# The delta rule's outputs kept token by token instead of feature by feature

## What is computed

```python
def step(s, xs):                      # one chunk of 64 tokens, per head, per direction
    qd, kd, u_c, w_c, qk_c, al = xs   # qd = q * exp(cumsum(log decay))
    v_new = u_c - w_c @ s
    o = qd @ s + qk_c @ v_new
    s = s * al + kd.T @ v_new
    return s, o

def finish(o_pair, gate):             # the two directions' outputs, latent tokens only
    o = rms_norm(o_pair[0] + o_pair[1], norm_g)     # over the 128 features of a head
    return (o * silu(gate)) @ w_out
```

## Time and profile before

| | |
|---|---|
| runs shown | 3884.72, 3899.01, 3894.75 us; median 3894.75 us |
| profiled execution | span 3889.4 us from the first to the last instruction; no separate time is given for it |
| TensorE busy | 3713.0 us, 95% |
| VectorE, ScalarE, GpSimd busy | 50%, 39%, 22% |
| mean granted TensorE clock | 0.980 |
| first scan, second chunk stage, second scan | about 255 to 461, 461 to 595, 595 to 804 us |
| gate, output projection | about 804 to 871, 871 to 919 us |

### The profile page before, as it was taken

One profiled execution on the slowest core, in us unless ns is written; L12 is line 12 of the kernel. 1 busy time (PEld: TensorE's weight loads), 2 busy tenths in 40 slices (PEclk: granted clock), 3 DMA queues, 4 the chain that ended last, 5 costly groups with the idle time before them and its releaser, 6 DMA issues.

```text
span 3889.4 us, 60956 instructions
## 1 busy us (share of the span) xinstructions
PE 3713.0 (95%) x25674; PEld 3011.8 (77%) x25674; DVE 1933.2 (50%) x2996; ACT 1516.2 (39%) x2548; POOL 845.8 (22%) x842
## 2 busy tenths in 40 slices
PE   6999899999999999998999999999999899999999
PEld 4678787987888757786888788876778688878887
DVE  6656555535444565745243543447565533454343
ACT  5533233323323356735233432235575522343222
POOL 1222122121111133442110120203344321002120
PEclk8999999989999999999999999999999999999999
DMA  6310030012222202111224122221111122222222
GB/s 240 121 43 3 19 70 3 3 64 105 97 96 96 71 28 76 61 60 49 94 96 137 63 93 98 98 82 39 66 60 60 35 96 98 103 92 98 95 96 91
DMA packets 81543, 300.88 MB, mean 77 GB/s; under 512 B 8824, under 2 KB 9976, under 8 KB 80504
## 3 DMA queue, kind: packets, MB, share of 16 engines
q1 hardware_dynamic: 80240, 294.90, 21.8%
q10 hardware_dynamic: 1032, 2.10, 0.5%
HBM read 292.76 MB, written 4.19 MB: 76 GB/s over the span
## 4 chain that ended last, share of the span: by engine, by line
PE 74%; DVE 11%; ACT 6%; issue 5%; POOL 3%; DMA 1%; SPq 0%; DVEq 0%; POOLq 0%; ACTq 0%
PE ps L208 73%; DVE wlo L239 1%; DVE he L247 1%; ACT whi L227 1%; DVE ac L247 1%; PE ps L213 1%; ACT ha L227 1%; POOL p L243 1%; DVE hc L2476 1%; ACT L227 1%; ACT wp L228 1%; DVE ss L247 1%; DVE ws L247 1%; DVE ha L239 1%; DVE sml L1944 0%
## 5 line engine op out<-in xcount | busy, mean ns | idle before, releaser
L239 DVE TENSOR_TENSOR wlo<-wraw,whi 128x1024 fp32r<-128x1024 f32 x537 | 689.8, 1289 | 777.4 <-ACT whi L227 776.7
L208 PE MATMUL ps<-hh,whi 128*128 128x512 f32 x1840 | 732.0, 398 | 6.5 <-ACT hh L227 2.1
L208 PE MATMUL ps<-hl,whi 128*128 128x512 f32 x1840 | 722.6, 393 | 0.0
L208 PE MATMUL ps<-hh,wlo 128*128 128x512 f32 x1840 | 722.0, 392 | 0.0
L227 ACT ACTIVATE whi<-wraw 128x1024 fp32r<-128x1024 f32 x537 | 559.6, 1049 | 207.7 <-PE ps L208 171.8
L208 PEld LDWEIGHTS ps<-hh,whi 128*128 128x128 f32 x1840 | 348.9, 190 | 90.9 <-ACT hh L227 7.7
L208 PEld LDWEIGHTS ps<-hh,wlo 128*128 128x128 f32 x1840 | 349.1, 190 | 74.2
L208 PEld LDWEIGHTS ps<-hl,whi 128*128 128x128 f32 x1840 | 349.5, 190 | 70.2
L208 PE MATMUL ps<-u,u 64*64 64x64 f32 (+2 forms) x6016 | 223.7, 226 | 25.5 <-DVE u L239 15.4
L208 PEld LDWEIGHTS ps<-u,u 64*64 64x64 f32 (+1 forms) x6016 | 204.7, 137 | 41.6 <-DVE u L239 19.4
L239 POOL TENSOR_TENSOR sml<-sml,con 128x4 f32<-128x4 f32 (+3 forms) x36 | 66.4, 1847 | 640.3 <-DVE sml L244 579.1
(11 more groups left out here) (402 smaller groups left out, 7062.6 us busy)
## 6 DMA issues: line engine op xcount, KB each, us to landing
wraw<-weights SPq DMA_DIRECT2D x537, 512.0 KB, 3.2
x<-xT SPq DMA_DIRECT2D x2, 2048.0 KB, 9.5
bias_lines<-ln ACTq DMA_DIRECT2D x1, 2048.0 KB
xmf<-memT SPq DMA_DIRECT2D x2, 1024.0 KB, 4.7
out<-x SPq DMA_DIRECT2D x4, 512.0 KB, 2.6
bias<-bias_lines SPq DMA_DIRECT2D x1, 1536.0 KB, 8.3
con<-consts SPq DMA_DIRECT2D x1, 1379.0 KB, 16.5
ctxt<-ctxT SPq DMA_DIRECT2D x1, 1024.0 KB, 18.4
```

The lines of the kernel that those rows point to most:

```text
L208: self.last, self.open = self.e.matmul(out, lhsT, rhs, start=start, stop=stop, skip_group_check=skip), True
L239: return self.e.tensor_tensor(out, a, b, op)
```

## The change

Outputs are now made with tokens on the partitions. The q product uses q itself as the weights and the state as the moving operand, into the rows of its chunk; the decay is applied afterwards, as a scale per partition on ScalarE while it leaves PSUM (into `EQ`), and GpSimd adds it to `OT`. The score product goes to a PSUM bank of its own, one for both directions. `OT` is laid out by unit pair (`place`), with 128 tokens by 512 features. The squares of head group 0 are made in the q steps of the second chunk stage, on ScalarE, and summed in the free dimension on VectorE; GpSimd takes the root and normalizes. Those of group 1 are made at the gate, where VectorE normalizes. TensorE transposes `OT` there, four transposes a head, and VectorE does the whole gating in two instructions, which also put the tokens back in order. The input is reloaded in four parts. The core of the diff:

```diff
@@ pe_scan
             elif ph == "qk":
-                b = K.ps.take(pe, "gq", *z)
-                for h in hs:
-                    pe.mm(H(b, h), K.col(K.gg, s, hg, h).broadcast_to([128, 128]), inc)
-                pe.mark("gq", *z)
...
                 if lat:
-                    b = [K.ps.take(pe, "o", *z, d) for d in range(2)]
-                    pe.wait_ge(pool.at("q", *z))
+                    b = K.ps.take(pe, "os", *z)
                     for h in hs:
                         for d, hf, c in pair:
-                            pe.mm(Q(b[d], h), H(K.SS[:, d, :], h), EQ[:, h * 128 + hf * 64:h * 128 + hf * 64 + 64], h == 0, False,
-                                  skip=True)
+                            pe.mm(H(b, h)[rows[hf], :], K.QT[:, h, (c - 4) * 64:(c - 3) * 64], H(K.SS[:, d, :], h))
...
-                    b = [K.ps["o", hg, s, d] for d in range(2)]
+                    b = K.ps.take(pe, "o", *z)
                     pe.wait_ge(act.at("vn", *z), act.at("pt", *z))
                     for h in hs:
-                        for d, hf, c in pair:
-                            pe.mm(Q(b[d], h), H(BA, h)[rows[hf], :], Q(PP, h)[rows[hf], :], False, h == 3, skip=True)
+                        for r in rows:
+                            pe.mm(H(b, h)[r, :], Q(PP, h)[r, :], H(BA, h)[r, :])
@@ act_scan (the exponential of "gq" goes; at "vn")
+                for h in hs if lat else ():
+                    act.wait_ge(pe.at("os", *z))
+                    act.a(H(EQ, h), H(K.ps[("os", *z)], h), ACT.Copy, scale=K.col(K.ex[:, 0], s, hg, h)).then_inc(act("eq", *z), 1)
@@ act_scan, dve_scan, pool_scan at "out"
+                    act.cp(K.OT[:, K.place(s), hg, :], K.ps[("o", *z)]).then_inc(act("o", hg, K.place(s)), 1)
...
+                    dve.wait_ge(pe.at("o", *z), pool.at("o2", hg, K.place(s)))
+                    dve.tt(dst, dst, K.ps[("o", *z)], ALU.add).then_inc(dve("o", hg, K.place(s)), 1)
...
+                    pool.wait_ge(act.at("eq", *z), act.at("o", hg, j) if s < 8 else pool.at("o1", hg, j))
+                    pool.tt(dst, dst, EQ, ALU.add).then_inc(pool("o1" if s < 8 else "o2", hg, j), 1)
@@ pool_scan
-            elif ph == "qk":
-                for d, hf, c in K.pair(s):
...
-                    pool.tt(v, v, K.QT[:, :, (c - 4) * 64:(c - 3) * 64], ALU.mult).then_inc(pool("q", *z), 1)
@@ act_chunks, dve_chunks, pool_chunks (second head group, kind q)
+                    act.wait_ge(dve.at("o", 0, i))
+                    act.a(K.OT[:, i, 1, :], K.OT[:, i, 0, :], ACT.Square).then_inc(act("osq", 0, i), 1)
...
+                    K.dve_osum(0, i, K.OT[:, i, 1, :])
...
+                        K.pool_oroot(0, i)
...
+                        pool.tt(o, o, bcl(K.ov[:, 1, 0, i, :], 128), ALU.mult).then_inc(pool("on", 0, i), 1)
@@ new helpers
+    def dve_osum(self, hg, j, squares):
...
+        dve.e.reduce_sum(o[:, 0, hg, j, :], squares.rearrange("p (a b) -> p a b", b=128), AXX).then_inc(dve("osum", hg, j), 1)
...
+        dve.ts(o[:, 0, hg, j, :], o[:, 0, hg, j, :], 1.0 / 128, ALU.mult, EPS, ALU.add).then_inc(dve("ort", hg, j), 1)
+    def pool_oroot(self, hg, j):
...
+        pool.tt(o[:, 1, hg, j, :], o[:, 0, hg, j, :], K.con("mhalf").broadcast_to([128, 4]), ALU.pow).then_inc(pool("oroot", hg, j), 1)
@@ pe_gout
-                pe.mm(b[:, h * 4 + c:h * 4 + c + 1], K.OSQ[:, h, c * 128:c * 128 + 128], K.con("ones")[:, 0:1])
...
+        def turn(h):
+            b = K.ps.take(pe, "or", h)
+            for p, j in ((2, 3), (1, 2), (3, 1), (0, 0)):
+                pe.wait_ge(K.dve.at("on", 1, j) if h >= 4 else K.pool.at("on", 0, j))
+                pe.tr(b[:, p * 128:p * 128 + 128], K.OT[:, j, h // 4, h % 4 * 128:h % 4 * 128 + 128], K.con("id"))
+            pe.mark("or", h)
...
+            K.proj(("og", h), K.wkey(3072 + h * 128), [(K.ps.take(pe, "og", h), K.lat)])
+            if h > 0:
+                turn(h - 1)
@@ act_gout (the copy to YHI of head h - 1 now follows the sigmoid of head h)
+        for j in (3, 2, 1, 0):
+            act.wait_ge(K.dve.at("o", 1, j), [x.at("unit", 1, 8) for x in K.lines])
+            act.a(K.OSQ[:, j, :], K.OT[:, j, 1, :], ACT.Square).then_inc(act("osq", 1, j), 1)
@@ dve_gout (four sums at h = 0, four normalizations at h = 1; the gating of h - 1 follows the product of h)
+            for hf, turned in enumerate((slice(None), slice(None, None, -1))):
...
+                dve.stt(halves[0], halves[1][:, turned, :], K.vec("gng"), ALU.mult, halves[2], ALU.mult).then_inc(dve("oy", h), 1)
@@ pool_gout
-            pool.tt(s3, K.T1[(h,)], K.T2[(h,)], ALU.mult).then_inc(pool("oy", h), 1)
@@ sync
-                K.load("x2", K.x, d["xT"], dve.at("on", 7), dve.at("osq", 6), act.at("osq", 7))
+                for j in range(4):
+                    K.load(f"x2_{j}", K.x[:, 2 * j:2 * j + 2, :], d["xT"][:, 2 * j:2 * j + 2, :], pe.at("or", 7), act.at("osq", 1, j))
```

More of the change, by code:

```diff
@@ L1258, in dve_chunks @@
                 dve.also(f"zb{hg}", *z)
+                if hg == 1 and kind == "q":
+                    K.dve_osum(0, i, K.OT[:, i, 1, :])
             elif kind == "v" or step == 3:
@@ L1325, in unit, with place @@
         return s % 2, s >= 4, self.units[s % 4]
+    def place(self, s):
+        return s - 4 if s < 8 else 11 - s
     def cols(self, t, s, hg):
@@ L1599, in pe_gout @@
-        pe.mark("osum")
-        sm = K.sml["o",]
-        for h in ks8:
-            bg, br = K.ps.take(pe, "og", h), K.ps.take(pe, "or", h)
-            K.proj(("og", h), K.wkey(3072 + h * 128), [(bg, K.lat)])
-            pe.wait_ge(K.pool.at("oroot"))
-            for c in range(4):
-                pe.mm(br[:, c * 128:c * 128 + 128], sm[:, h * 4 + c:h * 4 + c + 1].broadcast_to([128, 128]), K.con("id"))
-            pe.mark("or", h)
-        pe.also("sml", "o")
+        def turn(h):
[4 more added lines that the diff above has]
+            pe.mark("or", h)
@@ L1616, in act_gout @@
         K, act = self, self.act
-        for h in range(1, 8, 2):
-            act.wait_ge(K.ended("scan", 1))
-            act.a(K.OSQ[:, h, :], K.OT[:, h, :], ACT.Square).then_inc(act("osq", h), 1)
+        for j in (3, 2, 1, 0):
+            act.wait_ge(K.dve.at("o", 1, j), [x.at("unit", 1, 8) for x in K.lines])
+            act.a(K.OSQ[:, j, :], K.OT[:, j, 1, :], ACT.Square).then_inc(act("osq", 1, j), 1)
         for h in ks8:
@@ L1631, in act_gout, with act_yhi, gated @@
         act.mark("end", "gout")
+    def act_yhi(self, h):
+        K, act = self, self.act
+        act.wait_ge(K.dve.at("oy", h), K.ended("scan", 1))
+        act.cp(K.YHI[:, h, :], K.T3[(h,)]).then_inc(act("oyh", h), 1)
+        act.also("t3", h)
     def dve_gout(self):
         K, dve, pe = self, self.dve, self.pe
-        dve.wait_ge(K.ended("scan", 1))
-        for h in range(0, 8, 2):
-            dve.tt(K.OSQ[:, h, :], K.OT[:, h, :], K.OT[:, h, :], ALU.mult).then_inc(dve("osq", h), 1)
-        sm = K.sml.take(dve, "o")
-        dve.wait_ge(pe.at("osum"))
-        dve.ts(sm[:, 32:64], K.ps["osum",][:, 0:32], 1.0 / 128, ALU.mult, EPS, ALU.add).then_inc(dve("ort"), 1)
-        dve.also("ps", "osum")
+        def gated(h):
+            s3 = K.T3.take(dve, h)
+            dve.wait_ge(pe.at("or", h), dve.at("osl", h))
+            for hf, turned in enumerate((slice(None), slice(None, None, -1))):
+                halves = [x.rearrange("p (a b i) -> p a b i", b=2, i=64)[:, :, hf, :] for x in (s3, K.ps["or", h], K.T1[(h,)])]
+                dve.stt(halves[0], halves[1][:, turned, :], K.vec("gng"), ALU.mult, halves[2], ALU.mult).then_inc(dve("oy", h), 1)
+            dve.also("ps", "or", h)
+            dve.also("t1", h)
         for h in ks8:
             K.dve_feed("og", h)
-            s1, s2 = K.T1[(h,)], K.T2.take(dve, h)
+            if h == 0:
+                for j in (3, 2, 1, 0):
+                    K.dve_osum(1, j, K.OSQ[:, j, :])
+            if h == 1:
+                for j in (3, 2, 1, 0):
+                    o = K.OT[:, j, 1, :].rearrange("p (a b) -> p a b", b=128)
+                    dve.wait_ge(K.pool.at("oroot", 1, j))
+                    dve.tt(o, o, bcl(K.ov[:, 1, 1, j, :], 128), ALU.mult).then_inc(dve("on", 1, j), 1)
+            s1 = K.T1[(h,)]
             dve.wait_ge(K.act.at("osg", h))
```

80 lines of the change are left out of this document (38 added, 42 removed).

## The result

The changed kernel takes **3843.51 us** (median of 4 runs, 3842.06 to 3853.68) against 3896.88 us of the kernel before beside it (4 runs, 3884.72 to 3899.77): ratio 0.9864, 95% interval 0.9846 to 0.9882. So the change saves 53 to 58 us. The forecast was 3848 us, in its range; its sum was 46.7 us, too small by some 8 us.

What follows compares the result with a forecast made beforehand. TensorE's work was taken as the bound; scan -30, gate -19 and second chunk stage +2.3 sum to -46.7 us, from the 3889.4 us span to 3842.7, forecast as 3848 us with the runs' 5.35 us, range 3826 to 3868.

Steps and rivals of the forecast that it cites:

- The bound: Whole kernel: TensorE, busy 95% of the span, bounds it; other engines' chains share the bound in drains and q steps.
- the prediction's two prices: Scan, TensorE, each of 16 units: 1.09 us for the dropped decay spread, 0.91 us for the q product's new shape.
- Scan, -30 us: Both scans: 32.0 us of TensorE work go, plus up to 3 us of bank waits; taken as 30, ends 27 and 35.
- Half lost: Rival, scan: TensorE waits for VectorE's state updates in every unit, so half the cut is lost; 3863 us, chance 0.14.
- wholly absent: Rival, scan: the chain from state to state sets the time, so the scan's cut is all lost; 3878 us, chance 0.03.
- The other engines: Scan: added ScalarE copies (1.6 us), GpSimd and VectorE work hidden; last outputs complete about 1 us later, TensorE not waiting.
- ScalarE as the slower rival: Rival, scan: scaled copies of 2 us each overrun ScalarE's gap and delay the transposed copy; +80, 3928 us, chance 0.03.
- Second chunk stage, +2.3 us: Q steps: GpSimd's power and broadcast product delay each root, so TensorE leaves 2.3 us late; ends 0 and +8.
- The gate, -19 us: Gate: sums of squares 15.4, lower clock 1.6, transposes for spreads 2.9 us go, less new-chain latency; ends 15 and 22.
- the stalls of 0.2, 0.5 and 0.3 us: Gate: new chain's latency, 0.2 and 0.5 us for second projection and fourth's weight split, 0.3 for the end.
- The clock rival: Rival, gate: transposes between projections let the clock fall, so projections run at 1.2 GHz; 3892 us, chance 0.05.
- The base: Whole kernel: profiled span of 3889.4 us, plus 5.35 us by which the median of the runs lay above it.

Runs made afterwards that it cites:

- E1: Changed kernel with the four decay-spread products put back into a PSUM bank nobody reads: 3861.98 us against 3843.51 us.
- E3: Changed kernel with the product of q and state in its old shape, in one bank: 3865.9 us against 3843.51 us.
- E5: Kernel before, with the decay of q left out (no spread, exponential or GpSimd product): 3882.08 us, ratio 0.9952.
- E7: Changed kernel with 64 one-column product instructions, on data already there, put ahead of the first gate projection: 3860.61 us.
- E9: The changed kernel run again unaltered, as partner for three later runs: 3841.41 us against 3899.07 us of the kernel before.
- E4: Changed kernel with each of a unit's four scaled copies cut into eight of 16 columns: 3886.35 us.
- E11: Changed kernel with GpSimd's power and broadcast product of the first group's norm put behind the previous q step's root: 3845.12 us, ratio 0.9857.
- E6: Kernel before, with its 64 one-column sums of squares replaced by a single product of 32 columns: 3886.18 us, ratio 0.997.
- E12: E11's kernel, with GpSimd's output additions of units 6 and 7 also moved later: 3841.32 us, ratio 0.9851.
- E2: Changed kernel with the product of q and state issued twice into the same bank: 3857.1 us.
- E10: Changed kernel without the first head group's norm in the second chunk stage's q steps: 3838.32 us.

## Why the prediction held, point by point

- **The bound.** Right: TensorE's work is the time in the scan and at the gate. E1 and E3 return 1.09 and 0.91 us per unit, the prediction's two prices, to 0.03 us.
- **Scan, -30 us.** At the same clock it is the fall of the sum, 15.78, and 0.91 for the last q product: 16.69 a scan, 33.4 us. The term failed in its choice within its ends: the work was 32.0, another 0.9 a scan came on top, which E5 has with the decay and the prediction put on bank waits, and I took 2 us off for a drain with idle TensorE. Nothing was to be taken off. The drain is a chain on which the q product itself lies, and E3's price there, 0.93, is that of the middle, as I had written and then not used. "Half lost" and "wholly absent" are refuted by E1.
- **The clock in the scan**, which no step had. In the second scan of before 2.1 us more went than in the first: 0.69 at its start and 1.31 in its last period, both at a lower clock. They make the -18.79 out of -16.7. They are not the change's: E3, E7 and E9, made from the changed kernel, show such falls as well, and before's first scan shows none.
- **The other engines.** Right. Four scaled copies take 1.14 us, between the lower end of 0.6 and the 1.6 I took, since one starts 0.25 us behind the other though each lasts longer; the GpSimd addition takes 1.3 us; the last outputs come 1.5 us later against the last product, which itself ends 0.9 sooner.
- **ScalarE as the slower rival.** Its price is refuted by the trace and its mechanism shown by E4. A chance of 0.03 was fair: the distance to the row was a factor of 4.5.
- **Second chunk stage, +2.3 us.** The step is right in its place: the root's product starts 2.69 us later against the stage's start (26.12 against 23.43 us), 2.08 of it through the two GpSimd operations that I had put at 1.0 and 1.3. Its conclusion, that TensorE leaves the q steps as late as that, failed. Before, TensorE waits 1.83 us more at the next root, and loses clock behind that; after, this wait is gone, and the clock falls earlier. In the first k projection TensorE is 0.54 us late, behind a wait of 0.68 us for the next root 1.4, and the stage ends 0.82 us late. E11 shows the same from the other side: with the first wait at 0.89 again, the second becomes 2.68 us. A wait inside a chain that is bound elsewhere moves; it does not add. Here the stretch of low clock moved with it.
- **The gate, -19 us.** Measured -20.4. Sums and the waits around them 15.3 (15.4 predicted) and 1.7 of low clock (1.6); a head's period falls by 0.42 us where I had 0.36, 3.4 in all; and the stalls of 0.2, 0.5 and 0.3 us did not occur: TensorE is busy 47.70 of 47.70 us. Those were put in as caution, with no row behind them. Of the 15.3, E6 gives 11.2 to the products and leaves 4.1, mostly the wait under them, which the changed order removes since a projection stands there. About half of the products' 13.77 us is the lower clock: they start 0.21 us apart in before, from the first on, and 0.11 in E7 as long as the clock is at 1.00. In before it was low when they began, behind the scan's end and the wait of 1.65 us.
- **The clock rival**, 0.05. Refuted: with 32 and with 64 transposes among the projections the granted clock is 1.00 throughout. By the Trainium skill (TensorE: Matmul & The Clock Gate, Part 4: PE-mode transpose) a transpose took about 275 ns in one kernel and doesn't engage the full clock; here it takes 0.09 to 0.10 us and keeps it.
- **The base.** I added 5.35 us from the span to the median of three runs; 1.8 of it is fixed, the rest was the luck of that execution. Its start-up was the shortest of fourteen profiles, and over all comparisons the kernel before has medians of 3896.9 to 3900.0 us. That base too low by 2 to 5 us and the sum too small by 8 partly cancelled in the forecast.

## What to carry to other kernels

Where one engine's work is the time, price an edit by the distance of its neighbours' starts, and believe it in full, in the drain too, if the instruction lies on the chain. One-column products are a poor sum: 64 cost 13.6 us, about half of it through the lower clock that came with them; a sum in the free dimension on an engine with idle time, and a transpose later, cost next to nothing. Before two spans are compared, cut them at common instructions and set aside the stages that neither edit touched.

## What was unexpected in the hardware

- Start-up, the same code in fourteen profiles, takes 255.0 to 264.5 us. The runs of the changed kernel scatter by 6 to 12 us in a comparison.
- The granted clock at the end of a scan differs between executions of one program. The same drain (TensorE busy 18.2 of 22 us in after, 18.4 in E9) was followed by a clock of 1.00 in after and of 0.66 in E9's first scan. That cost 2.5 us; the other 1.9 us by which this scan is longer than E9's second stand ahead of its first q product. Windows of E9:

```profile
440.00:455.00 15.00, 11.98 (x165) 10.20 (x164) 5.32 (x16) 4.33 (x11) 2.36 (x2) 0.77 0.01 2
445.00:455.00 10.00, 8.40 (x85) 6.95 (x86) 1.78 (x6) 2.69 (x6) 1.09 (x1) 0.66 0.00 0
```

- Apart from the clock the scan repeats to 0.02 us (once 0.04) in every period, over executions and over the two scans of one, so that 0.35 us in one unit (E12) can be seen where the timed runs cannot tell 5 us.
- A group of sixteen products costs 1.09 us alone and 0.88 when it continues a group of its kind (E2).
- What makes the clock fall once or twice in the q steps (E10 against before) stays open.
